# A kernel's first normalization: the weight moved from rows to the turned tiles, and the first tile turned raw

## The reference, cut to what matters

```python
def rms_norm(x, g):
    xf = x.astype(jnp.float32)
    y = xf * lax.rsqrt(jnp.mean(xf * xf, axis=-1, keepdims=True) + EPS)
    return (y * g.astype(jnp.float32)).astype(x.dtype)
...
        n = rms_norm(h, g_mix[i])
        z = n @ w_in[i] + b_in[i]
        q, k, v, u, bg, cg, ga, gc = jnp.split(z, SPLITS, axis=-1)
```

## Time and profile before

| what | us |
|---|---|
| median of 3 runs | 1699.89 |
| lowest and highest | 1698.74, 1703.71 |
| the profiled execution's own time | 1703.22 |
| its span | 1701.4 |
| TensorE busy, share of the span | 98% |
| VectorE, ScalarE, GpSimd busy | 50%, 22%, 12% |

### The profile page before, as it was taken

How to read it: one execution, slowest core, us unless ns; L and a number is a source line. 1 busy time by engine, 2 the same in 40 slices (tenths; PEclk the granted TensorE clock), 3 DMA queues, 4 the chain that set the end, 5 groups by cost and what they waited for, 6 DMA issues and landing times.

```text
span 1701.4 us, 19747 instructions
## 1 busy us (share of the span) xinstructions
PE 1670.4 (98%) x7614; PEld 984.2 (58%) x7614; DVE 857.1 (50%) x1479; ACT 381.9 (22%) x686; POOL 211.4 (12%) x279
## 2 busy tenths in 40 slices
PE   7999999999999999999999999999999999999998
PEld 3887886765434343333334456688855544667664
DVE  3665843354523232322325446676756654677663
ACT  1112212001100000000002212321244433544530
POOL 2333410001100000000001000010234520000000
PEclk9999999999999999999999999999999999999999
DMA  7313113235799999999996123114120021212101
GB/s 292 118 56 124 50 56 128 99 149 202 291 421 426 427 427 427 426 426 427 426 425 269 47 78 123 51 61 154 73 99 2 1 75 49 100 50 75 75 1 50
DMA packets 28001, 308.63 MB, mean 181 GB/s; under 512 B 4415, under 2 KB 4703, under 8 KB 10368
## 3 DMA queue, kind: packets, MB, share of 16 engines
q1 hardware_dynamic: 21456, 289.22, 41.9%
q0 software_dynamic: 6448, 18.10, 3.0%
HBM read 306.58 MB, written 4.19 MB: 183 GB/s over the span
## 4 chain that ended last, share of the span: by engine, by line
PE 92%; DVE 4%; DMA 2%; issue 1%; ACT 1%; POOL 0%; SPq 0%; DVEq 0%; ACTq 0%
PE ps L418 88%; PE ps L421 4%; DMA wring<-in_w 2%; DVE arena L1211 2%; ACT arena L2328 0%; DVE arena L1238 0%; DVE arena L1222 0%; DMA arena<-in_rows 0%; DVE small L1226 0%; POOL small L2764 0%; DMA wring<-in_dense 0%; DVE arena L1216 0%; DVE H L1211 0%; DVE arena L1298 0%; DVE ps L1211 0%
## 5 line engine op out<-in xcount | busy, mean ns | idle before, releaser
L418 PE MATMUL ps<-arena 128*64 128x512 f32 (+13 forms) x2384 | 513.8, 397 | 2.8 <-DVE arena L1238 1.1
L418 PEld LDWEIGHTS ps<-arena 128*64 128x64 f32 (+4 forms) x2384 | 231.4, 153 | 221.3 <-issue 214.6
L418 PE MATMUL ps<-wring,arena 128*64 128x512 f32 (+2 forms) x1048 | 345.1, 564 | 1.2 <-ACT arena L2328 0.7
L1211 DVE TENSOR_TENSOR arena<-ps,arena 128x512 f32<-128x512 f32 (+2 forms) x189 | 129.3, 684 | 421.7 <-PE ps L418 266.6
L418 PE MATMUL ps<-wring,HT 128*128 128x512 f32 (+1 forms) x880 | 313.4, 508 | 4.1 <-ACT HT L2328 1.9
L418 PEld LDWEIGHTS ps<-wring,HT 128*128 128x128 f32 x880 | 164.5, 191 | 126.8 <-issue 113.6
L418 PE MATMUL ps<-HT,wring 128*128 128x512 f32 (+2 forms) x656 | 222.1, 501 | 0.0
L2328 ACT ACTIVATE arena<-ps 128x512 f32<-128x512 f32 (+4 forms) x155 | 82.8, 534 | 597.5 <-PE ps L421 304.9
L418 PE MATMUL ps<-wring 128*128 128x256 f32 x864 | 195.7, 380 | 0.0
L418 PEld LDWEIGHTS ps<-wring,arena 128*64 128x64 f32 (+1 forms) x1048 | 131.4, 151 | 88.0 <-issue 83.1
L418 PEld LDWEIGHTS ps<-wring 128*128 128x128 f32 x864 | 162.3, 190 | 23.9 <-issue 2.6
(11 more groups left out here) (120 smaller groups left out, 961.9 us busy)
## 6 DMA issues: line engine op xcount, KB each, us to landing
wring<-in_w SPq DMA_DIRECT2D x48, 2048.0 KB, 21.0
wring<-in_dense SPq DMA_DIRECT2D x38, 2048.0 KB, 8.1
arena<-in_w SPq DMA_DIRECT2D x36, 2048.0 KB, 19.6
HT<-in_w SPq DMA_DIRECT2D x12, 2048.0 KB, 17.9
arena<-in_rows POOLq DMA_DIRECT2D x29, 256.0 KB, 4.4
H<-in_x SPq DMA_DIRECT2D x4, 512.0 KB, 5.4
wring<-in_dense SPq DMA_DIRECT2D x2, 1024.0 KB, 5.9
arena<-in_relb POOLq DMA_DIRECT2D x8, 256.0 KB, 8.6
```

The costliest lines, as they stand in the source:

```text
L418: return nc.tensor.matmul(o, l, r, start=start, stop=stop, skip_group_check=True)
L1211: done(nc.vector.tensor_tensor(o, a, b, op), tell)
```

## The change

The weight g_mix is no longer a row. It is a constant of eight columns, one for each k, which comes with the identity (138 columns instead of 130), and stands feature by partition. It is applied where the transposed tiles are copied from PSUM to HT: by ScalarE in four instructions of 128x128 with a scale for each partition, instead of one of 128x512; by VectorE in one multiplication instead of one copy. The multiplication by 1/rms alone is one instruction of 128x1024 on VectorE (`scaled`) instead of two of 128x512.

Tile 0 is transposed twice. First it is transposed as it is in H ("R"), ahead of its sum of squares, weighted, and used for its q; its bank is multiplied by 1/rms in the same instruction that adds b_q. Later it is transposed again as a normed tile ("A", 0), for the other products. The tiles come in the order 1, 0, 2, 3 in `nbs`.

SP loads the first half of w_q third, with no wait; the second half waits for the first alone; x tiles 2 and 3 are issued right behind it; w_k waits for the second half as before. The two loads of g_mix rows, 256 KB each, are gone. GpSimd's rows 4 and 5 (b_k, b_v) no longer wait for a row buffer to be given back.

```diff
@@ constants
-for _n, _w in (("ident", 128), ("mhalf", 1), ("mone", 1), ("mqk", 128), ...
+for _n, _w in (("ident", 128), ("mhalf", 1), ("mone", 1), ("g_mix", 8), ("mqk", 128), ...
-ROWSEQ = (["g_mix", "g_mix+", "b_q", "misc", "b_k", ...
+ROWSEQ = (["", "", "b_q", "misc", "b_k", ...
@@ TensorE, turn and stage_a
-                v_ = nbs[i % 2].rearrange("t (p k) -> t k p", k=8)
+                v_ = nbs[(1, 0, 0, 1)[i] if nm == "A" else i % 2].rearrange("t (p k) -> t k p", k=8)
...
-                turn("A", 0)
+                pe.wait_ge(S("x0"), 16)
+                v_ = H[:, 0, :].rearrange("t (p k) -> t k p", k=8)
+                for j in range(2):
+                    f = fill(("t", "R", 0, j))
+                    for k in range(4):
+                        ins = tr(f.ap[:, k * 128:k * 128 + 128], v_[:, 4 * j + k, :])
+                    ins.then_inc(f.full, 1)
...
-                        if j and i < 3:
-                            turn("A", i + 1)
+                        if j:
+                            for x in ((1,), (0, 2), (3,), ())[i]:
+                                turn("A", x)
...
-                        evacuated(("t", "A", i, j))
+                        evacuated(("t", "A" if i else "R", i, j))
@@ VectorE, stage_a
-                g = row("g_mix"), row("g_mix+")
-                for i in range(4):
-                    stat(i, *g)
-                    if i == 1:
-                        turned("A", 0)
-                        turned("A", 1)
-                    elif i == 3:
-                        turned("A", 2)
+                nrow("row", 2)
+                gm = C("g_mix")[:, 4:8].unsqueeze(2).to_broadcast([128, 4, 128])
+
+                def weighted(nm, i):
+                    f = full("t", nm, i, 1)
+                    tt(HT[:, 4:8, i * 128:i * 128 + 128], f.ap.rearrange("p (k t) -> p k t", k=4), gm, MUL, f)
+
+                def scaled(i, at):
+                    heard("inv", at)
+                    ts(nbs[(1, 0, 0, 1)[i]], H[:, i, :], small[:, 4 + i:5 + i], None, MUL, tell="nb")
+                v.wait_ge(S("ident"), 16)
+                weighted("R", 0)
+                scaled(1, 2)
+                v.wait_ge(S("x0"), 16)
+                scaled(0, 0)
+                weighted("A", 1)
+                scaled(2, 1)
+                weighted("A", 0)
+                scaled(3, 1)
                 v.wait_ge(S("con"), 16)
...
-                    tt(zq[:, i, :], f.ap, r[1], ADD, f)
-                    if i == 1:
-                        turned("A", 3)
+                    if i:
+                        tt(zq[:, i, :], f.ap, r[1], ADD, f)
+                    else:
+                        stt(zq[:, i, :], f.ap, small[:, 4:5], r[1], MUL, ADD, f)
+                    if i == 0:
+                        weighted("A", 2)
+                    elif i == 1:
+                        weighted("A", 3)
@@ ScalarE, stage_a
+                def weighted(nm, i):
+                    f = full("t", nm, i, 0)
+                    for k in range(4):
+                        act(HT[:, k, i * 128:i * 128 + 128], f.ap[:, k * 128:k * 128 + 128], ACT.Identity, f if k == 3 else "a",
+                            scale=C("g_mix")[:, k:k + 1])
                 for i in range(4):
                     a.wait_ge(S(f"x{i}"), 16)
-                    if i > 1:
-                        full("t", "A", i - 2, 1)
-                    stat(i)
-                    if i == 1:
-                        turned("A", 0)
-                        turned("A", 1)
-                turned("A", 2)
-                turned("A", 3)
+                    act(sga[:, 2, :], H[:, i, :], ACT.Square, "rt", scale=1.0 / 32, accum_out=small[:, i:i + 1])
+                    if i == 0:
+                        a.wait_ge(S("ident"), 16)
+                        weighted("R", 0)
+                for i in (1, 0, 2, 3):
+                    weighted("A", i)
@@ GpSimd, row
-                    if n >= NR:
+                    if n >= NR + 2:
@@ SyncE
-            sp.dma_start(con[:, 0:130], T["con"][:, 0:130]).then_inc(S("ident"), 16)
-            for n in range(2):
-                sp.dma_start(rowbuf[n], T["rows"][ROWS["g_mix"] + n, :].partition_broadcast(128)).then_inc(S(f"gmix{n}"), 16)
+            sp.dma_start(con[:, 0:138], T["con"][:, 0:138]).then_inc(S("ident"), 16)
+            w, src = wslot[PLACE["w_q"][0]], T["dense"][DENSE.index("w_q")]
+            sp.dma_start(w[:, 0:2048], src[:, 0:2048]).then_inc(S("wq"), 16)
             sp.dma_start(H[:, 1, :], xv[:, 1, :]).then_inc(S("x1"), 16)
...
-            sp.wait_ge(S("gmix0"), 16)
-            sp.dma_start(w[:, 0:2048], src[:, 0:2048]).then_inc(S("wq"), 16)
-            sp.wait_ge(S("gmix1"), 16)
+            sp.wait_ge(S("wq"), 16)
             sp.dma_start(w[:, 2048:4096], src[:, 2048:4096]).then_inc(S("w0"), 16)
-            sp.wait_ge(S("w0"), 16)
             for i in (2, 3):
                 sp.dma_start(H[:, i, :], xv[:, i, :]).then_inc(S(f"x{i}"), 16)
+            sp.wait_ge(S("w0"), 16)
             load("w_k")
             sp.dma_start(pcl[:, :], T["pcl"]).then_inc(S("pcl"), 16)
-            sp.dma_start(con[:, 130:], T["con"][:, 130:]).then_inc(S("con"), 16)
+            sp.dma_start(con[:, 138:], T["con"][:, 138:]).then_inc(S("con"), 16)
```

More of the change, by code:

```diff
@@ L23 @@
 _c = 0
-for _n, _w in (("ident", 128), ("mhalf", 1), ("mone", 1), ("mqk", 128), ("mst", 128), ("c01", 128), ("rst", 512), ("ustr", 128), ("ones", 128),
+for _n, _w in (("ident", 128), ("mhalf", 1), ("mone", 1), ("g_mix", 8), ("mqk", 128), ("mst", 128), ("c01", 128), ("rst", 512), ("ustr", 128), ("ones", 128),
                ("sel", 512), ("iota", 512), ("tok", 4), ("cos", 32), ("sin", 32), ("ccos", 8),
@@ L42 @@
 _r = 0
-for _n, _w in (("b_q", 1), ("b_k", 1), ("b_v", 1), ("g_mix", 2), ("g_ffn", 2), ("g_ple", 2),
+for _n, _w in (("b_q", 1), ("b_k", 1), ("b_v", 1), ("g_ffn", 2), ("g_ple", 2),
                ("g_n0", 2), ("g_n1", 2), ("b_ple", 2), ("b_mv", 1), ("b_mo", 1), ("b_mz", 1), ("hn0", 1), ("b_nq", 1),
@@ L55 @@
 DENSE += ["o_o0", "o_o1"]
-ROWSEQ = (["g_mix", "g_mix+", "b_q", "misc", "b_k", "b_v", "misc", "g_ffn", "g_ffn+",
+ROWSEQ = (["", "", "b_q", "misc", "b_k", "b_v", "misc", "g_ffn", "g_ffn+",
            "g_ple", "g_ple+", "b_ple", "b_ple+", "g_n0", "g_n0+", "b_mv", "misc", "b_mo", "hn0", "b_mz", "misc", "b_nq",
@@ L1246, in row @@
                 assert ROWSEQ[n] == name, (n, ROWSEQ[n], name)
-                if n < 2:
-                    v.wait_ge(S(f"gmix{n}"), 16)
-                else:
-                    v.wait_ge(S(f"row{n % NR}"), 16 * (n // NR + (n % NR > 1)))
+                v.wait_ge(S(f"row{n % NR}"), 16 * (n // NR + (n % NR > 1)))
                 return n, rowbuf[n % NR]
@@ L2928, in load @@
                 sp.dma_start(wslot[s], src).then_inc(S(f"w{s}"), 16)
-            w, src = wslot[PLACE["w_q"][0]], T["dense"][DENSE.index("w_q")]
-            sp.wait_ge(S("gmix0"), 16)
-            sp.dma_start(w[:, 0:2048], src[:, 0:2048]).then_inc(S("wq"), 16)
-            sp.wait_ge(S("gmix1"), 16)
+            sp.wait_ge(S("wq"), 16)
             sp.dma_start(w[:, 2048:4096], src[:, 2048:4096]).then_inc(S("w0"), 16)
-            sp.wait_ge(S("w0"), 16)
             for i in (2, 3):
                 sp.dma_start(H[:, i, :], xv[:, i, :]).then_inc(S(f"x{i}"), 16)
+            sp.wait_ge(S("w0"), 16)
             load("w_k")
             sp.dma_start(pcl[:, :], T["pcl"]).then_inc(S("pcl"), 16)
-            sp.dma_start(con[:, 130:], T["con"][:, 130:]).then_inc(S("con"), 16)
+            sp.dma_start(con[:, 138:], T["con"][:, 138:]).then_inc(S("con"), 16)
             for key in ORDER_A[2:] + ORDER_B[:14]:
@@ L3012, in pack @@
     put("ident", np.eye(128))
+    put("g_mix", f["g_mix"][0].reshape(128, 8))
     put("mqk", np.where(p[None, :] <= p[:, None], 0.0, NEG))
@@ L3081, in pack @@
     pr("b_v", bi[1024:1536])
-    pr("g_mix", f["g_mix"])
     pr("g_ffn", f["g_ffn"])
```

## The result

| what | before | after |
|---|---|---|
| median of 17 runs each, us | 1702.27 | 1706.86 |
| lowest and highest, us | 1698.74, 1704.10 | 1704.27, 1708.62 |
| the profiled execution's own time, us | 1703.22 | 1708.62 |
| its span, us | 1701.4 | 1706.7 |

The changed kernel takes 1.0028 times as long, with a 95% interval of 1.0021 to 1.0034: 4.6 us more. The forecast was 1697.5 us in a range of 1694.0 to 1701.3, so the time lies outside it and on the other side of no change. The loss is a little smaller than the 0.3% under which the prediction called two times the same, but the interval lies wholly above 1, so the loss is real. Of the miss of 9.4 us, 2.4 come from the level: the three runs that the prediction started from had a lower median (1699.89) than the 17 (1702.27).

What follows compares the result with a forecast made beforehand. The prediction took TensorE, on the chain for 92% of the span, as the bound. Start -5.2, extra transposes +0.9 and the bank's wait +1.9 gave a gain of 2.4 us, from 1699.89 to 1697.5, range 1694.0 to 1701.3.

Steps and rivals of the forecast that it cites:

- (1): At the start: w_q's first half, issued third, lands at about 7.2 us, so q starts 5.2 us earlier.
- Rival (D): At the start: w_q's half lands at 9.7 us, sharing engines with x tile 1; 1697.5 to 1698.5; chance 0.50 including the forecast.
- (2): Tile 0's first transposes: ScalarE's four weightings take 1.3 us and are done at 6.9, before w_q lands.
- (3): q's first eight records: at the low clock they take the same 5.95 us as before, instead of 3.43.
- (4): Tile 1's scaling: x tile 1 lands near 8.6 us, scaled by 11.9, ahead of TensorE's need at 13.2.
- (5): Tile 0's second transposes: 0.88 us extra on TensorE; without further waits the third tile's q starts at 26.1, gain 4.3.
- (6): Tile 1's weighting on ScalarE, behind all four squares, ends at 18.7 us, wanted at 17.5; third tile's q at least 27.4.
- (7): Third tile's q waits for VectorE to empty ps2 behind `con`, landing at 27.2 us; start 28.0, wait +1.9.
- The term for `relb`: In `con`'s landing: POOL's tables, issued earlier, move 0.43 MB more ahead of it, +1.1 us.
- Rival (B): At the third tile's q: `con` lands after 29.3 us and nothing is gained; 1699.8 to 1701.2; chance 0.14.
- Rival (C): q's first tiles: the clock stays low, third tile's q 9.9 us later, about 1709.8; chance 0.06 with other losses over 5.1.
- What follows keeps its slack: Behind the third tile's q: later work and loads move along, VectorE's work stays the same within 1 us, under cover.

Runs made afterwards that it cites:

- the kernel with quarters: w_q's first half loaded as two quarters with a semaphore each, against the changed kernel with con's wait later and the banks' ring turned back: 1699.41 us, 0.9987.
- the ring's experiment: The kernel before with only its ring of PSUM banks moved on by two ahead of w_k's first product: 1706.01 us, 1.0026.
- the ring back: The changed kernel with its ring of PSUM banks moved on by six ahead of w_k, so later fills have their earlier banks: 1703.9 us, 1.0011.

## Why the prediction was wrong, step by step

**The bound** was read rightly: before, the chain lay on TensorE from the first product, and with both new waits taken away the gain ahead of w_k (1.8 us) stays to the end. One reading was off without consequence: behind the wait of 9.8 us it named the 0.6 us for w_q as next, but the view has waits of up to 1.1 us between the two.

**(1) w_q at 7.2: wrong, 9.7.** The step let the half's 1.05 MB stream at the full rate, 2.5 us, from 3.9 us on. The stream ran at half of that from 4 to 6 us, and with the identity issued behind the half and not ahead it lands at 6.74, inside the step's bounds. Rival (D) had the time (9.7) but gave x tile 1 as the reason, of which no more than 0.35 us is seen, and held that the late landing "costs little", since `con` would set the pace. Once `con` doesn't, it costs the later start in full, since q begins at 9.77 and not at 7.2.

**(2) ScalarE's four weightings: 1.57 us against 1.3.** Too small by 0.3, under cover of w_q's wait. **(3) The clock: right.** Eight records took 6.24 us against 5.95 (5.4 to 6.6 in the other kernels); weight loads come 0.86 us apart until 15 us. **(4) Tile 1 in time: right.** x tile 1 was in use at 10.98 instead of 8.6, and from its square to VectorE's scaling it took 2.16 us against 2.13. **(5) The transposes: right**, 0.88 us for eight. Without its wait, the third tile's q would start at 25.81 + 3.43 = 29.2 us in the kernel after (28.8 with the wait moved), not at 26.1. The difference is step 1's 2.6 us and some tenths of step 3. So the start alone gains 1.2 to 1.8 us, not 4.3.

**(6) The wait for ScalarE: right in kind.** Tile 1's weighting ran from 18.87 to 20.44, forecast 17.4 to 18.7. TensorE was late itself and waited 0.17 us only. In the kernel with quarters this wait grows to 1.7 us.

**(7) The bank behind `con`: the right wait, mis-sized.** `con` landed at 31.16, not at 27.2. 2.9 us of that come from w_q's second half (15.06, not 12.2), of which 2.5 follow step 1 and 0.4 are its own (5.32 us for the assumed 4.93). The remaining 1.1 us are in the corrections: -2.6 + 1.3 + 1.1 = -0.2 were forecast, and +0.9 is measured (16.10 against 15.17). The term for `relb` was mis-sized. It is a difference against before, where 0.21 MB (some 0.5 us) went ahead of `con`, so the measured 2.85 stands for 2.3 against the forecast 1.1. The others together are then 13.25 - (15.17 - 0.5) = -1.4 against -1.3: right. Without the tables and rows the wait is gone. "DMA: Bandwidth & Descriptors", section "Queues, rings and completion order", of the Trainium skill says that each engine takes packets from its queues in turn. The prediction read that as half of the stream, +3.4, which is as far above 2.3 as the forecast 1.1 is below it: GpSimd's queue moved 0.98 MB of 4.73 up to `con`, and not 1.57 MB. Rival (B)'s condition, `con` after 29.3, was met, and the new wait took the gain and more (E was 31.98, above its 31.7). (B) had 0.14.

**After the wait, the clock.** Rival (C) feared the low level through q's first tiles. It came elsewhere: behind the 2.6 us wait at 31.98, where the eight records took 5.37 us and not 3.43, +1.9. No step priced what a wait does to the clock after it. The start thus lost 1.5 us (31.98 against 30.43) and 1.9 us, together 3.5.

**"What follows keeps its slack": the step that failed altogether.** The order of instructions showed the first bank that moved, ps0 to ps2, and the prediction drew on it for step 7. It didn't see that the same counter moves every later bank by two, and put the cost of that at nothing. The one place where this turn meets a bank still in use costs 2.6 us, or 4.5 with the clock behind it. Of the loss of 4.6 us against the 2.4 us of forecast gain, a difference of 7.0, the ring is about 3 to 4 (2.8 and 4.1 by the medians), the late w_q and `con` with the clock behind their wait the rest. Both of its signs of being wrong came: the third tile's q after 30 us, and something later than 100 us that moves against the rest. None of its cases had a loss between 1.3 and 5.1 us, where the result lies.

**What stays open.** Near 1088 us the clock drops, with only 0.38 us of waiting ahead of it, in before, in the ring's experiment on it, with the quarters and with w_q first; in before it costs 1.7 us. In the other traces it doesn't drop there. Behind the late wait of 2.56 us it falls in the kernel after and with `con` first, and not with the wait for `con` moved, with the tables held, or in the ring's experiment on before. Behind the early wait it falls both times (2.6 us, and 3.0 with the ring back). What decides between the equal waits wasn't found; it is not the wait's length alone. Open too is why w_q's first packets are slow right behind the identity at the start.

## What to carry to other kernels

A fill more in a ring of banks that the whole program shares is a change to every later bank: compare the banks at all stage boundaries, where a burst of results is emptied late, and give the ring back its phase if one is hit. An operation that is moved ahead of others takes its bank's wait with it, so ask what stands in the emptying engine's queue ahead of the emptying; a wait that stands there for a load needed only later should move to where the load is needed. A start made earlier is worth only what the next load allows, and what a small load ahead of it costs can't be read from its bytes: 69 KB ahead of w_q's half cost 2.5 us, and ahead of x tile 1 nothing that shows.

## What the runs showed of the hardware that was not expected

A load of 128 rows of 552 bytes, issued between x tile 0 and one of 1.05 MB, made the latter land 2.5 us later (9.26 against 6.74), with the stream at 188 and 221 GB/s instead of 401 and 388 in the windows from 4 to 6 us. The same rows ahead of x tile 1 left it at 398 and 447. The load of 1.05 MB took 5.06 us from its issue when it was the first of all. After waits of TensorE of 2.6 to 3.0 us the granted clock fell to 0.50 in four of seven cases and cost 1.7 to 1.9 us, two thirds of the wait once more. Four `relb` tables and two rows on GpSimd's queue held a load on SP's back by 2.85 us, and up to its landing moved 0.98 MB of 4.73.
